# Expert outputs of the first block scattered by GpSimd three tiles later, and the second tile's tokens fetched by a gather

## The reference, cut to what matters

```python
def hier_moe(h, w_rg, b_rg, w_re, b_re, w_gate, w_up, w_down):
    p_group = jax.nn.softmax((h @ w_rg + b_rg).astype(f32), -1)
    g_idx, g_prob = jnp.argmax(p_group, -1), jnp.max(p_group, -1)
    e_logits = (h @ w_re + b_re).reshape(bsz, s, N_GROUPS_MOE, EXPERTS_PER_GROUP)
    e_in_group = jnp.take_along_axis(e_logits, g_idx[..., None, None], axis=2)[..., 0, :]
    top_logits, top_idx = lax.top_k(e_in_group, TOP_K_IN_GROUP)
    top_w = jax.nn.softmax(top_logits, -1) * g_prob[..., None]
    ...
    for e in range(N_EXPERTS):
        hid = jax.nn.silu(h @ w_gate[e]) * (h @ w_up[e])
        y = y + gates[..., e:e + 1] * (hid @ w_down[e])
    return y
```

## Time and profile before

| | |
|---|---|
| median of 3 runs | 1459.01 us |
| profiled execution's own time | 1457.84 us |
| its span | 1455.9 us |
| PE busy | 1248.0 us, 86% |
| VectorE, ScalarE, GpSimd busy | 48%, 32%, 29% |
| DMA, mean | 180 GB/s |
| first routing, begin to end | about 300 to 322 us |
| first expert stage | about 323 to 485 us |
| second routing | about 1179 to 1199 us |
| second expert stage | about 1200 to 1432 us |

### The profile page before, as it was taken

The page is one execution under the profiler, slowest core; times in us unless marked ns, Lnnn a source line. Parts: engine busy times, 40 slices in busy tenths (PEclk is TensorE's granted clock), DMA queues, the critical chain, the costliest instruction groups (busy, mean ns, idle before and its releaser), DMA issues. The chain is left out here.

```text
span 1455.9 us, 25454 instructions
## 1 busy us (share of the span) xinstructions
PE 1248.0 (86%) x10212; PEld 959.7 (66%) x10216; DVE 701.6 (48%) x1273; ACT 463.3 (32%) x1015; POOL 418.7 (29%) x354
## 2 busy tenths in 40 slices
PE   7998768969999159899999999999788969997871
PEld 6776446868887148758979978778676855553430
DVE  5797783554444555662754637682124352111112
ACT  4533243233333244442342243423222321121110
POOL 5354311211110214212414234234334302332223
PEclk9998979989999669999999999999999989999996
DMA  7300183159996603101121313322122499999985
GB/s 273 105 11 1 52 296 148 44 195 359 372 387 260 214 7 129 60 2 65 58 89 62 112 34 113 118 87 66 51 85 93 195 408 412 417 419 420 420 371 186
DMA packets 64918, 261.97 MB, mean 180 GB/s; under 512 B 8226, under 2 KB 18082, under 8 KB 52000
## 3 DMA queue, kind: packets, MB, share of 16 engines
q1 hardware_dynamic: 54176, 233.73, 42.2%
q0 software_dynamic: 8832, 20.36, 4.0%
q10 hardware_dynamic: 1792, 6.29, 1.2%
HBM read 240.73 MB, written 29.43 MB: 186 GB/s over the span
## 5 line engine op out<-in xcount | busy, mean ns | idle before, releaser
L1712 POOL TENSOR_TENSOR block_w_lo<-block_w,block_w_hi 128x512 fp32r<-128x512 f32 x96 | 130.2, 1358 | 210.0 <-ACT block_w_hi L1690 210.0
L2432 PE MATMUL e_gu<-e_w,r_xT 128*64 128x256 f32 x896 | 104.6, 387 | 18.9 <-DMA e_w<-in_gu 17.0
L251 PE MATMUL dil_bank<-block_w_hi,xT_hi 128*128 128x512 f32 x288 | 116.3, 404 | 4.4 <-PEq L842 4.4
L1690 ACT ACTIVATE block_w_hi<-block_w 128x512 fp32r<-128x512 f32 x96 | 60.4, 631 | 178.4 <-PE dil_bank L253 114.5
L253 PE MATMUL dil_bank<-block_w_hi,xT_lo 128*128 128x512 f32 x288 | 114.4, 397 | 0.0
L252 PE MATMUL dil_bank<-block_w_lo,xT_hi 128*128 128x512 f32 x288 | 114.3, 397 | 0.0
L2432 PEld LDWEIGHTS e_gu<-e_w,r_xT 128*64 128x64 f32 x896 | 63.0, 138 | 51.9 <-DMA e_w<-in_gu 19.1
L251 PEld LDWEIGHTS dil_bank<-block_w_hi,xT_hi 128*128 128x128 f32 x288 | 77.9, 270 | 8.5 <-issue 4.7
L252 PEld LDWEIGHTS dil_bank<-block_w_lo,xT_hi 128*128 128x128 f32 x288 | 78.1, 271 | 3.8
L253 PEld LDWEIGHTS dil_bank<-block_w_hi,xT_lo 128*128 128x128 f32 x288 | 77.7, 270 | 3.9
L2494 DVE TENSOR_TENSOR e_prod<-e_sg,e_gu 128x128 f32<-128x128 f32 x32 | 9.2, 288 | 137.5 <-ACT e_sg L2526 137.5
(11 more groups left out here) (512 smaller groups left out, 3071.1 us busy)
## 6 DMA issues: line engine op xcount, KB each, us to landing
e_w<-in_gu SPq DMA_DIRECT2D x44, 2048.0 KB, 27.0
e_w<-in_dn SPq DMA_DIRECT2D x48, 1024.0 KB, 28.1
block_w<-in_w_dil SPq DMA_DIRECT2D x9, 2048.0 KB, 8.1
block_w<-in_w_out SPq DMA_DIRECT2D x4, 2048.0 KB, 9.2
block_w<-in_w_gates SPq DMA_DIRECT2D x4, 2048.0 KB, 11.0
w_t<-in_w_in_t SPq DMA_DIRECT2D x12, 512.0 KB, 3.7
slot_rows<-blank SPq DMA_DIRECT2D x12, 512.0 KB, 5.9
slot_rows<-e_y ACTq DMA_DIRECT2D x16, 384.0 KB, 9.7
```

The lines of the kernel that those rows point to most:

```text
L251: pe.matmul(out, lhs[0], rhs[0], start=first, stop=False)
L1690: act.activation(wh[:, j % RING, 0:width[i]], k.w[:, slot, c, 0:width[i]], ACT.Copy).then_inc(hi_ready, 1)
L1712: pool.tensor_tensor(wl[:, j % RING, 0:width[i]], k.w[:, (q0 + i) % 2, c, 0:width[i]], wh[:, j % RING, 0:width[i]].bitcast(F32), ALU.subtr ...
L2432: ins = pe.matmul(gubank[t % 2][g * S:(g + 1) * S, 0:2 * FG], xT[t % 2][:, turned_at(c):turned_at(c) + S], w1_piece(slot.of[t], w, 2 * FG) ...
```

## The change

Four edits go together.

1. In the first expert stage `y` is no longer stored by ScalarE. GpSimd copies the tile's column of a new table `y_of` (the row of `slots` for each slot, or a number past the end for a slot without a token) and issues an indirect DMA that scatters only rows with a token. It does this in tile t for tile t-3 (LATE = 3), behind the gather of tile t.
2. In both routings the PE picks rows for tile 0 only. Tile 1 is gathered by GpSimd as its first instruction of the expert stage, and transposed by the PE in tile 0, behind the up product in the first block and behind gate and up in the second.
3. In the first block the weights of slot 3 are loaded in the routing block, with those of slot 2.
4. The zeros cover all 3072 rows of `slots`: 24 DMAs.

```diff
@@ route
-                def pick_rows(i):
-                    pe.wait_ge(first_ready, i + 1)
...
-                pick_rows(0)
+                pe.wait_ge(first_ready, 1)
+                for c in range(KD):
...
-                pick_rows(1)
...
-                step(dve.scalar_tensor_tensor(first_rank[:], ranks[:, :, 0:2], 1.0, M[:, :, 0:2], ALU.add, ALU.mult))
+                step(dve.scalar_tensor_tensor(first_rank[:], ranks[:, :, 0], 1.0, M[:, :, 0], ALU.add, ALU.mult))
...
+                step(dve.tensor_scalar(empty[:], tbank[0:GROUPS * S, 0:NT], -0.5, float(NO_ROW), ALU.is_gt, ALU.mult))
@@ experts, GpSimd
+                def put_y(i, b):
+                    t, g = R * i + b, b % 2
+                    if isinstance(t, int) and t == 0:
+                        pool.wait_ge(k.routed, 1)
+                    if not isinstance(t, int) or t >= 2:
+                        pool.wait_ge(y_out[g], 16 * pair(i, b))
+                    pool.tensor_copy(y_idx[g][:], k.y_of[:, bass.ds(t, 1)]).then_inc(y_idx_ready[g], 1)
+                    pool.wait_ge(y_idx_ready[g], pair(i, b) + 1)
+                    pool.wait_ge(y_v, t + 1)
+                    pool.wait_ge(y_s, t + 1)
+                    pool.sem_inc(y_seen, 1)
+                    pool.indirect_dma_start(out_rows, bass.IndirectOffsetOnAxis(ap=y_idx[g][:], axis=0), y[g][:], None,
+                                            bounds_check=SLOTS - 1, oob_is_err=False).then_inc(y_out[g], 16)
...
+                    if not isinstance(t, int) or t >= LATE:
+                        put_y(i, b - LATE)
...
+                pool.indirect_dma_start(xg[1][:], None, rows, bass.IndirectOffsetOnAxis(
+                    ap=k.tok_of[:, 1:2], axis=0), bounds_check=SEQ - 1, oob_is_err=False).then_inc(x_in[1], 16)
@@ experts, PE
                     half(t, b, ubank, FF // P, gu_done)
+                    if isinstance(t, int) and t == 0:
+                        turn_x(1, 1, 0)
@@ experts, ScalarE
-                    act.wait_ge(y_s, t + 1)
-                    act.wait_ge(y_v, t + 1)
-                    act.dma_start(out_rows[bass.ds(t * S, S), :], y[b % 2][:]).then_inc(y_out[b % 2], 16)
@@ experts_moving, PE
-                    if more is not None and t >= 1:
+                    if more is not None:
                         with more(t + 1):
                             turn_x(t + 1)
@@ first_block
-            first = min(E1 * S1, E2 * S2)
-            spare = d["slots"][first:, :].rearrange("(n p) (a f) -> n p a f", p=P, f=256)
+            spare = d["slots"].rearrange("(n p) (a f) -> n p a f", p=P, f=256)
...
-            first_loads(sp, weights, range(2, 3), d["gu1"], d["dn1"])
+            first_loads(sp, weights, range(2, W_SLOTS), d["gu1"], d["dn1"])
```

More of the change, by code:

```diff
@@ L1884, in _ @@
                         pe.wait_ge(oh_ready, i + 1)
-                    for g in range(1 if k.y_of is None else 2):
+                    for g in range(GROUPS):
                         ins = pe.matmul(tbank[g * S:(g + 1) * S, 0:NT], ohr[:, i, tt, :], ohj[:, i, tt, :], start=(j == 0),
@@ L1899, in _ @@
                 act.activation(gap_exp[:], gap[:], ACT.Exp).then_inc(exp_ready, 1)
[L1900 to L1904, removed]
+                act.wait_ge(picked_x, 1)
+                for h in range(2):
+                    act.activation(k.xT[0][:, h * XH:(h + 1) * XH], pick[h][:, 0:XH], ACT.Copy).then_inc(xT_ready, 1)
             @block.vector
@@ L1988, in rest_of_routing @@
         step = Chain(dve, routed_step)
-        if k.y_of is not None:
-            step(dve.scalar_tensor_tensor(empty[:], k.c("iota")[:, 0:NT], 2.0 * S, empty[:], ALU.mult, ALU.add))
+        step(dve.scalar_tensor_tensor(empty[:], k.c("iota")[0:GROUPS * S, 0:NT], float(GROUPS * S), empty[:], ALU.mult, ALU.add))
+        if GROUPS == 1:
+            step(dve.tensor_scalar(k.y_of[:], empty[:], k.c("tok")[0:S, 0:1], float(NO_TOKEN), ALU.add, ALU.add))
+        else:
             step(dve.tensor_scalar(k.y_of[:], empty[:], k.c("half_row"), None, ALU.add))
@@ L2016, in __call__, with experts @@
         return self.eng.If(self.used > t)
-def experts(k, name, E, S, x_in, rows, w_gu, w_dn, out_rows, weights, late, tail):
+def experts(k, name, E, S, x_in, rows, w_gu, w_dn, out_rows, weights, tail):
     nc = k.nc
@@ L2098, in extra @@
                         load(e, i, b)
-                first_loads(sp, weights, late, w_gu, w_dn)
                 tail.load(sp)
@@ L2212, in tile @@
                     step = one_by_one(t)
-                    if not isinstance(t, int) or t >= 1:
-                        with more(t + 1):
-                            copy_x(t + 1, b + 1)
+                    with more(t + 1):
+                        copy_x(t + 1, b + 1)
                     dve.wait_ge(w2_hi, t + 1)
```

70 lines of the change are left out of this document (37 added, 33 removed).

## The result

Seven runs of the changed kernel gave 1463.28 to 1471.6 us, median 1465.28; seven of the kernel before 1452.2 to 1459.05, median 1457.23. The ratio is 1.0063 with a 95% interval of 1.0047 to 1.0079: 9.2 us slower (6.8 to 11.5). The forecast was 1457.3.

What follows compares the result with a forecast made beforehand. First expert stage: PE bounds early tiles, the weight stream late ones; the second stage is the stream's. Terms -2.4 - 8.0 + 9.0 - 0.6 + 0.3 = -1.7 on 1457.84, plus 1.2 for the median: 1457.3 us, range 1449 to 1469.

Steps and rivals of the forecast that it cites:

- (d): First expert stage, GpSimd: the scatter ahead of the next gather delays it; twelve gathers cost 9.0 us, ends 0 and 14.
- L: Time until a gather in the first expert stage lands, taken as 10.4 us.
- w: Lengthening of each first-stage tile by the late gather, (11.9 + L - 20.8) / 2, taken as 0.75 us.
- third rival, held gather: First expert stage, tiles 4 to 15: scatter holds the gather in GpSimd's queue, L = 12.5, 1469.9 us; chance 0.20.
- (b): Start of first expert stage: tile 1 must be fetched, yet gate 2 comes 2.4 us earlier, between 0.5 and 4.4.
- (c): First block: tile 3's weights issued in the routing, and scatters costed cheaper, end waits for the weight stream; gain 8.0 us.
- (a): First routing: without the second tile's row picking the block is shorter and the first gate starts 5.9 us earlier.
- (f): Beside the first attention: 24 zero stores instead of 12 stay hidden by 2.9 us; cost 0, ends 0 and 2.
- (g): Second block: second pick goes, tile 1 waits for a gather under a full DMA; cost 0.3 us, ends 0 and 2.
- (e): Tail of the first expert stage: last y to the combine gather takes 4.87 us instead of 5.47; gain 0.6.

Runs made afterwards that it cites:

- late4: The changed kernel with the first block's scatter four tiles later instead of three; ratio 0.9994 (0.9984 to 1.0004) against the kernel before.
- b_w3: The kernel before with only the fourth slot's weights issued early, in the routing; ratio 0.9971 (0.9958 to 0.9984) against the kernel before.
- w3_late: The changed kernel with the fourth slot's weights issued in the expert stage again, not the routing; ratio 1.0096 (1.0079 to 1.0113) against the kernel before.

## Why the prediction was wrong

*What failed is step (d), the price of the scatter in front of the gather*: 9.0 us were taken, 12.1, 14.0 and 14.9 are measured, mean 13.7 (gates 2 to 15 of the three profiles less 118.5, the mean of late4's two). The mechanism was right in its parts: the gather starts 2.82 us into the next tile, offset 11.84 where 11.9 was worked out; the PE waits for it at the transposes; nobody waits for weights. What was mis-sized is L. I had all landings of this stage at hand, 10.1 to 12.0 with median 11.2, and took 10.4 on the argument that a longer tile empties the DMA. It does (0.92 for 1.00), and the landing between 337 and 470 us stayed at 11.0 (11.5 in the third profile). With 11.0 the same formula gives w = 1.0 and 12.2 us, and the first profile has 12.1; with 11.2 it gives 13.8. My own third rival said "It decides from L = 11", and the median already at hand lay above that. The formula also had no term for the clock that can fall behind such a wait, though my step (b) counted that very thing for the first gate. The PE's waits for a gather and 1.6 us for each low clock add up to what was lost in each profile: 12.0 + 0, 10.2 + 4.8, 12.3 + 1.6.

*The second step that failed is the size of (c).* 8.0 us were to be gained between the third and the last gate. The measured gain is 6.0: 124.5, the mean of the four profiles with the stage of before, less 118.5. The profile I read, with 125.3, was the longest of the four, and 1.7 us of it were not the stream's length but low clock behind a wait for weights (last section). And in late4, with no wait for weights left, some tiles take 9.4 to 9.6 us, so the 13 intervals need 118.5 and not 117.3.

*The held gather* (0.20) gave the sign but not the cause: it wanted L = 12.5 from the queue. That 1465.3 lies inside the stated range of 1449 to 1469 is owed to this rival's part of it, for the forecast's own range ended at 1463; it is luck. By the Trainium skill, "DMA: Bandwidth & Descriptors", section "Queues, rings and completion order", which says it of SyncE's and ScalarE's queues, each DMA engine takes up the descriptors of a ring in order, and a later one may still finish its write before an earlier one. No run here shows what happens within the queue; the landing with and without the scatter ahead, 11.0 and 11.1, shows no price of it.

*Right.* (a), and (b) by its number: gate 0 follows 5.3 to 6.3 us earlier on the memset than the 20.3 of before, gate 2 by 1.4 to 2.9, where 2.4 was said; but b_w3, which picks both tiles, gets 1.2 there by the early weights alone, which I had counted only between the gates. (f): nothing. (g): 1.4 in the mean of four, within the 0 to 2 given, each of the four being too uncertain to say more.

*Small misses.* (e) was to gain 0.6 and loses 0.7: from the last gate to the combine gather it is 19.3 us in all three profiles of the changed kernel and 18.6 in the mean of the four with the stage of before. The scatter starts 0.90 us behind y, as costed (0.86), but from its start to the combine gather it is 4.9 us, where I had taken the 4.0 of the second block:

```profile
480.87 0.69 DVE L2228 COPY e_y<-e_ybank 96x512 f32<-96x512 f32 x1 [3.13 <-PE e_ybank L253]
482.46 0.93 POOL L2122 DMA_INDIRECT slot_rows<-e_y,e_y_idx  x1 [4.50 <-DVE e_y L2228]
487.38 0.98 POOL L2627 DMA_INDIRECT e_w<-slot_rows,r_slot  x1 [4.00 <-POOLq L2146]
```

*The sum.* By the profiles the stretch is 6.4 us longer (mean of three, 187.3, against 180.9): -2.0 to gate 2, +7.7 between the gates (late4 has -6.0 there, the scatter's place the other 13.7), +0.7 behind them. The forecast for the same stretch was -2.4 - 8.0 + 9.0 - 0.6 = -2.0. Of the 8.4 us between the two 4.7 are (d), 2.0 are (c), 1.3 are (e) and 0.4 are (b). The timed 9.2 has 6.8 at its lower end; the rest is the second block's 1.4 and what can't be told from chance.

## What to carry to other kernels

Work moved to an in-order engine is paid by what stands behind it there. Ask of each moved instruction when its data are whole and when the next one's were: here the scatter's came 6 us after the gather's condition, and one tile more of lateness (late4) took the whole price away. Once a transfer is late at all, every further microsecond of its landing is paid (here by half, in each tile), so a small error in the landing is a large one in the sum: take the median that the stage shows, not its quick end, and a term for the low clock that can follow the waits.

A part that gains alone may be worth less beside a new bound, and show its worth again when the bound goes: the early weights gave 7.4 us of the stretch by themselves, and 2.4 beside the late scatter, none of them between the third and the last gate.

## What the runs showed of the hardware

- In the second profile of the changed kernel the clock fell to 1.2 GHz behind the PE's wait of 3.08 us and behind two shorter ones (2.16 and 1.98 us), 1.6 us lost at each; in the first profile, with ten waits of 0.16 to 2.17 us, it stayed at 2.4 GHz between the third and the last gate. The length of the wait alone doesn't decide: w3_late has a wait of 3.07 us at 355.31, and its granted clock from 352 to 364 us is 1.00. Nor is it the change's alone. The kernel before has one such place in its first profile and none in its second: the gate below took 4.51 us for 2.81, and the clock from 416 to 421 us was 0.66.

```profile
416.15 4.51 PE L2152 MATMUL e_gate<-r_xT,e_w 128*64 128x96 f32 x64 [1.97 <-DMA e_w<-in_gu]
```

- An indirect gather for 96 slots (rows of 4 KB, on average 64 slots hold a token) takes 10.7 to 11.5 us in the median from issue to landing beside the weight stream, between 337 and 470 us of every profile that gives it: 11.2 where the DMA share is 1.00 (before), 10.8 where it is 0.90 with a scatter of as many rows 4 us ahead in the same queue (late4), 11.0 with one 2 us ahead (after).
